# Cached-value transfers, the last cached-key scores and the last mixing product of a cross-attention stage, reordered

## The reference, cut to what matters

```python
qh = q.reshape(b, L, MEM_HEADS, MEM_HEAD_DIM)
scores = einsum('blhd,bmhd->bhlm', qh, mem_k) * MEM_HEAD_DIM ** -0.5
probs = softmax(scores, axis=-1)
o = einsum('bhlm,bmhd->blhd', probs, mem_v).reshape(b, L, MEM_DIM)
y_m = o @ w_mem_out
merged = g[:, :, 0] * y_a + g[:, :, 1] * y_b + g[:, :, 2] * y_m   # g = sigmoid of the gate projection
mix = merged @ w_o
```

## Time and profile before

| what | value |
|---|---|
| median of three runs | 1590.66 us (1589.77 to 1594.83) |
| the profiled execution, its own time | 1599.25 us |
| its span from first to last instruction | 1597.2 us |
| TensorE busy | 1478.5 us, 93% of the span |
| VectorE, ScalarE, GpSimd busy | 692.6, 455.4, 187.6 us |
| bytes moved | 368.26 MB, mean 231 GB/s |
| chain that ended last, by engine | PE 74%, DMA 17%, DVE 4%, ACT 2%, issue 2% |
| mean granted clock of TensorE | 0.969 of full speed |

### The profile page before, as it was taken

The page is one execution under the profiler, slowest core; times in us unless marked ns, Lnnn a source line. Parts: engine busy times, 40 slices in busy tenths (PEclk is TensorE's granted clock), DMA queues, the critical chain, the costliest instruction groups (busy, mean ns, idle before and its releaser), DMA issues.

```text
span 1597.2 us, 34713 instructions
## 1 busy us (share of the span) xinstructions
PE 1478.5 (93%) x14399; PEld 1190.5 (75%) x14399; DVE 692.6 (43%) x1246; ACT 455.4 (29%) x870; POOL 187.6 (12%) x360
## 2 busy tenths in 40 slices
PE   7999999999999999999999989979987887997896
PEld 7999999999988999999988769754543443443442
DVE  5766576675789472223444325564111111111114
ACT  4533545445322551223343333111100000000001
POOL 1100000000000000000000000003333233333322
PEclk9999999999999999999999989979998998999998
DMA  5232445434558332262455452966999999999994
GB/s 203 67 92 79 129 128 164 135 102 145 171 205 281 104 93 93 80 226 84 128 193 183 178 215 83 402 250 263 419 423 422 422 421 422 380 412 421 420 410 178
DMA packets 87394, 368.26 MB, mean 231 GB/s; under 512 B 14296, under 2 KB 37536, under 8 KB 72800
## 3 DMA queue, kind: packets, MB, share of 16 engines
q1 hardware_dynamic: 81120, 357.37, 59.1%
q0 software_dynamic: 6144, 8.95, 1.6%
HBM read 344.81 MB, written 29.31 MB: 234 GB/s over the span
## 4 chain that ended last, share of the span: by engine, by line
PE 74%; DMA 17%; DVE 4%; ACT 2%; issue 2%; SPq 1%; POOL 0%; POOLq 0%; DVEq 0%; ACTq 0%
PE ps L638 36%; DMA arena<-in_w 16%; PE ps L1104 8%; PE ps L782 6%; PE ps L1123 4%; PE ps L996 3%; PE ps L887 3%; PE ps L869 3%; PE ps L733 1%; PE ps L730 1%; PE ps L919 1%; PE ps L898 1%; PE ps L1088 1%; PE ps L723 1%; PE ps L1164 1%
## 5 line engine op out<-in xcount | busy, mean ns | idle before, releaser
L1104 PE MATMUL ps<-arena,xT 128*32 128x256 f32 x4096 | 254.4, 400 | 66.7 <-DMA arena<-in_w 64.7
L1104 PEld LDWEIGHTS ps<-arena,xT 128*32 128x32 f32 x4096 | 131.7, 115 | 166.3 <-issue 53.9
L1650 DVE TENSOR_TENSOR wl<-raw,wh 128x1024 fp32r<-128x1024 f32 x151 | 183.4, 1222 | 160.5 <-ACT wh L1195 160.1
L638 PE MATMUL ps<-xh,wh 128*128 128x272 f32 x1136 | 244.2, 296 | 4.6 <-DVE wl L1650 3.4
L638 PE MATMUL ps<-xh,wl 128*128 128x272 f32 x1136 | 235.5, 289 | 0.0
L638 PE MATMUL ps<-xl,wh 128*128 128x272 f32 x1136 | 235.0, 288 | 0.0
L638 PEld LDWEIGHTS ps<-xh,wh 128*128 128x128 f32 x1136 | 179.6, 189 | 15.4 <-issue 9.7
L638 PEld LDWEIGHTS ps<-xl,wh 128*128 128x128 f32 x1136 | 179.2, 189 | 0.0
L638 PEld LDWEIGHTS ps<-xh,wl 128*128 128x128 f32 x1136 | 178.1, 189 | 0.0
L1195 ACT ACTIVATE wh<-raw 128x1024 fp32r<-128x1024 f32 x151 | 158.1, 1055 | 40.4 <-PE ps L996 20.8
L2337 DVE TENSOR_TENSOR hbuf<-sg,ps 128x128 f32<-128x128 f32 x64 | 18.4, 288 | 301.0 <-ACT sg L1502 218.1
(11 more groups left out here) (428 smaller groups left out, 2352.3 us busy)
## 6 DMA issues: line engine op xcount, KB each, us to landing
arena<-in_w SPq DMA_DIRECT2D x96, 2048.0 KB
raw<-in_slabs SPq DMA_DIRECT2D x151, 512.0 KB, 4.4
bc<-acs_dram SPq DMA_DIRECT2D x16, 512.0 KB, 5.8
hs<-in_h SPq DMA_DIRECT2D x16, 512.0 KB, 5.2
out_h_sample<-hs SPq DMA_DIRECT2D x16, 512.0 KB, 4.1
kv<-in_kT SPq DMA_DIRECT2D x8, 1024.0 KB, 4.9
kv<-in_vc SPq DMA_DIRECT2D x4, 1024.0 KB, 7.8
kvx<-in_vc SPq DMA_DIRECT2D x2, 2048.0 KB, 11.9
```

The source lines that it names most:

```text
L638: r = nc.tensor.matmul(ps[:, 2 * (ub % 2) + half, 0:HT], w[:, s, col], x[:, koff + kk, half * HT:half * HT + HT], start=first and kk == 0 ...
L1104: r = nc.tensor.matmul(ps[QS * c:QS * c + QS, 2, 0:2 * FQ], xT[:, s, kk % 2, kk // 2 * QS:kk // 2 * QS + QS], arena[:, at_:at_ + 2 * FQ], ...
L1650: v.tensor_tensor(wl[:, s], raw[:, s], wh[:, s].bitcast(F32), ALU.subtract).then_inc(w_lo, 1)
```

## The change

1. Values are used in the order 0 to 7. v0 goes into slots 2 and 3 of `raw` (`v_raw`), v1 into `kv[2]`, v2 into `kv[0]`, v3 into `kv[1]`, v4 to v7 into `kvx`. The first four are issued when slab M+7 has been split (v0), after the last `scores` (v1), after `sample_scores(6)` (v2) and after `sample_scores(7)` (v3). Slabs M+10 and M+11 are loaded after `sample_values(0)`.
2. `sample_scores(7)` runs inside gate slab M+7, after its fifth block. `gather_scores(7)`, `maximum(16)` and `softmax(16)` move into the last iteration on their engines; the sample probabilities stay in `otok`.
3. The last `mix_values` writes bank 5 and doesn't wait for `low_o(6)`. `turn(16)` stands between the last two mixing products, and VectorE does `own_p(0)` and `own_p(1)` ahead of `low_o(7)`.
4. The split and remainder of slab M+10 come after the last copy of the sample rows.

```diff
-V_ORDER = (0, 1, 3, 4, 5, 6, 2, 7)
+V_ORDER = (0, 1, 2, 3, 4, 5, 6, 7)
+        v_raw = raw[:, 2:4].rearrange("p s n -> p (s n)")
...
             for k in range(KT):
+                if k < KT - 2:
+                    load(S0["M"] + RING + k)
+                    sp_.wait_ge(Z["kvb_used"], k + 1)
+                    load_kv(k + 2)
+            sp_.wait_ge(w_lo, S0["M"] + RING + KT)
+            load_v(0, v_raw, "kvb_in2")
+            sp_.wait_ge(Z["sc_mm"], MH * CHUNKS)
+            sp_.wait_ge(Z["kvb_in2"], 16)
+            load_v(1, kv[2][:], "kvb_in2")
+            sp_.wait_ge(Z["kvb_used"], NSEQ - 1)
+            load_v(2, kv[0][:], "kvb_in0")
+            sp_.wait_ge(Z["kvb_used"], NSEQ)
+            load_v(3, kv[1][:], "kvb_in1")
+            sp_.wait_ge(w_free, RING + S0["M"] + KT)
+            for half in range(2):
+                sp_.dma_start(kvx[:, 2 * half:2 * half + 2],
+                              A["vc"][4 + 2 * half:6 + 2 * half].rearrange("b p f -> p b f")).then_inc(Z["mem_vc_in" if half else "a_vc_in"], 16)
+            sp_.wait_ge(Z["kvb_used"], NSEQ + 1)
+            for k in range(KT - 2, KT):
                 load(S0["M"] + RING + k)
-                sp_.wait_ge(Z["kvb_used"], k + 1)
-                if k < NSEQ - 2:
-                    load_kv(k + 2)
-                if k == NSEQ - 2:
-                    load_kv(NSEQ + 1)
-                    sp_.wait_ge(Z["sc_mm"], MH * CHUNKS)
-                    load_kv(NSEQ)
-                    sp_.wait_ge(w_free, RING + S0["M"] + KT)
-                    for half in range(2):
-                        sp_.dma_start(kvx[:, 2 * half:2 * half + 2],
-                                      A["vc"][3 + 2 * half:5 + 2 * half].rearrange("b p f -> p b f")).then_inc(Z["mem_vc_in" if half else "a_vc_in"], 16)
-                if k == NSEQ - 1:
-                    load_kv(NSEQ + 2)
-            sp_.wait_ge(Z["kvb_used"], NSEQ + 1)
-            load_kv(NSEQ + 7)
...
+            O_BANK = (7,) * (2 * MH - 1) + (5,)
...
-                    pe.wait_ge(Z["s_own"], min(it + 1, 2 * NSEQ))
+                    pe.wait_ge(Z["s_own"], it + 1 if it < NIT - 2 else 2 * NSEQ)
+                rows_ = prob[:, it % 2] if it < NIT else otok[:]
...
-                if 2 * h + d:
-                    pe.wait_ge(Z["o_lo"], 2 * h + d)
+                if 0 < n_ < 2 * MH - 1:
+                    pe.wait_ge(Z["o_lo"], n_)
...
-                pe.wait_ge(Z["s_own"], max(b + 1, 2 * b))
+                pe.wait_ge(Z["s_own"], max(b + 1, 2 * b) if b < NSEQ - 1 else 2 * NSEQ - 1)
...
-                gate_part(k, 2, KT)
+                if k < KT - 1:
+                    gate_part(k, 2, KT)
+                else:
+                    gate_part(k, 2, 5)
+                    sample_scores(k, 2 * k)
+                    gate_part(k, 5, KT)
...
-            sample_scores(KT - 1, 2 * KT)
             mix_values(MH - 1, 0)
+            turn(NIT)
             mix_values(MH - 1, 1)
-            turn(NIT)
...
             pe.wait_ge(Z["s_own"], 3 * NSEQ + 1)
+            pe.wait_ge(Z["o_lo"], 2 * MH)
...
                 split(b + 2)
+                if k == KT - 1:
+                    softmax(NIT, otok[:])
...
             high_o(2 * MH - 2)
-            softmax(NIT, otok[:])
+            turned(NIT, PTs[:].rearrange("p m h t -> p m (h t)"))
             high_o(2 * MH - 1)
-            turned(NIT, PTs[:].rearrange("p m h t -> p m (h t)"))
...
                 low(S0["M"] + k + 2)
+                if k == KT - 1:
+                    gather_scores(k)
+                    maximum(NIT, otok[:])
...
+            normalise(NIT)
             low_o(2 * MH - 2)
-            gather_scores(NSEQ - 1)
-            maximum(NIT, otok[:])
-            normalise(NIT)
+            dve.wait_ge(Z["pt_a"], NIT + 1)
+            own_p(0)
+            own_p(1)
             low_o(2 * MH - 1)
-            dve.wait_ge(Z["pt_a"], NIT + 1)
-            for b in range(NSEQ):
+            for b in range(2, NSEQ):
                 own_p(b)
```

More of the change, by code:

```diff
@@ L513, in load_kv, with load_v @@
             def load_kv(n_):
-                slot = n_ % 2 if n_ < NSEQ else {0: 2, 1: 0, 2: 1, 7: 2}[n_ - NSEQ]
-                sp_.dma_start(kv[slot][:], A["kT" if n_ < NSEQ else "vc"][n_ % NSEQ]).then_inc(Z[f"kvb_in{slot}"], 16)
+                sp_.dma_start(kv[n_ % 2][:], A["kT"][n_]).then_inc(Z[f"kvb_in{n_ % 2}"], 16)
+            def load_v(b, dst, landed):
+                sp_.dma_start(dst, A["vc"][b]).then_inc(Z[landed], 16)
             load_kv(0)
@@ L907, in turn @@
                 if it and it % 2 == 0:
-                    pe.wait_ge(Z["s_own"], min(it + 1, 2 * NSEQ))
+                    pe.wait_ge(Z["s_own"], it + 1 if it < NIT - 2 else 2 * NSEQ)
+                rows_ = prob[:, it % 2] if it < NIT else otok[:]
                 for m in range(2):
-                    r = nc.tensor.transpose(ps[:, 6, m * P:m * P + P], prob[:, it % 2, m * P:m * P + P], ident)
+                    r = nc.tensor.transpose(ps[:, 6, m * P:m * P + P], rows_[:, m * P:m * P + P], ident)
                 r.then_inc(Z["pt_mm"], 1)
             def mix_values(h, d):
+                n_ = 2 * h + d
                 pe.wait_ge(Z["pt_a"], CHUNKS * (h + 1))
-                if 2 * h + d:
-                    pe.wait_ge(Z["o_lo"], 2 * h + d)
+                if 0 < n_ < 2 * MH - 1:
+                    pe.wait_ge(Z["o_lo"], n_)
                 for m in range(2):
-                    r = nc.tensor.matmul(ps[:, 7, :], mv[:, m, h * MHD + d * P:h * MHD + d * P + P], PT[h % 2][:, m],
+                    r = nc.tensor.matmul(ps[:, O_BANK[n_], :], mv[:, m, h * MHD + d * P:h * MHD + d * P + P], PT[h % 2][:, m],
                                          start=m == 0, stop=m == 1)
@@ L936, in sample_values @@
                 b = V_ORDER[n_]
-                if 3 <= b < 7:
-                    if b < 5:
+                if b == 0:
+                    pe.wait_ge(Z["kvb_in2"], 16)
+                    values = v_raw
+                elif b == 1:
+                    pe.wait_ge(Z["kvb_in2"], 32)
+                    values = kv[2][:]
+                elif b < 4:
+                    pe.wait_ge(Z[f"kvb_in{b - 2}"], 16 * (NSEQ // 2 + 1))
+                    values = kv[b - 2][:]
+                else:
+                    if b < 6:
                         pe.wait_ge(Z["a_vc_in"], 48)
@@ L941, in sample_values @@
                         pe.wait_ge(Z["mem_vc_in"], 32)
[L942 to L946, removed]
+                    values = kvx[:, b - 4]
                 pe.wait_ge(Z["s_own"], 2 * NSEQ + n_ + 1)
@@ L1446, in _ @@
             r.then_inc(Z["g_done"], 1)
-            split(S0["M"] + KT + 2)
             act.wait_ge(Z["pt_mm"], NIT + 2)
@@ L1450, in _ @@
                                  ps[:, 5, 0:MEM].rearrange("p (d h t) -> p d h t", d=2, h=MH), ACT.Copy).then_inc(Z["o_hi"], 1)
+            split(S0["M"] + KT + 2)
             def high_merged(k):
@@ L2032, in normalise @@
                 c_.sync()
-                v.tensor_scalar(prob[:, it % 2], prob[:, it % 2], stat[:, 3, it:it + 1], None, ALU.mult).then_inc(Z["sm_p"], 1)
+                rows_ = prob[:, it % 2] if it < NIT else otok[:]
+                v.tensor_scalar(rows_, rows_, stat[:, 3, it:it + 1], None, ALU.mult).then_inc(Z["sm_p"], 1)
             def low_o(n_):
                 dve.wait_ge(Z["o_hi"], n_ + 1)
-                v.tensor_tensor(ol[:, n_, 0:SEQ], ps[:, 7, :], oh[:, n_, 0:SEQ].bitcast(F32), ALU.subtract).then_inc(Z["o_lo"], 1)
+                v.tensor_tensor(ol[:, n_, 0:SEQ], ps[:, 7 if n_ < 2 * MH - 1 else 5, :], oh[:, n_, 0:SEQ].bitcast(F32), ALU.subtract).then_inc(Z["o_lo"], 1)
             def own(buf, src, b, used):
@@ L2096, in _ @@
             v.tensor_copy(otok[:], ps[:, 4, 0:MHD]).then_inc(Z["s_own"], 1)
-            low(S0["M"] + KT + 2)
             dve.wait_ge(Z["o_hi"], 2 * MH + 1)
@@ L2101, in _ @@
                             oh[:].rearrange("p (h d) t -> p d h t", d=2)[:, :, :, SEQ:T].bitcast(F32), ALU.subtract).then_inc(Z["o_lo"], 1)
+            low(S0["M"] + KT + 2)
             dve.sem_inc(tmp_free, KT)
```

7 lines of the change are left out of this document (4 added, 3 removed).

## The result

| | median | runs | ratio to before (95% interval) |
|---|---|---|---|
| before | 1592.97 us (1589.77 to 1599.07) | 6 | |
| after | 1585.13 us (1582.56 to 1587.21) | 6 | 0.9945 (0.9929 to 0.9960) |
| after, run again later | 1585.86 us | 6 | 0.9950 (0.9934 to 0.9965) |

The change makes the kernel 8.8 us faster by the first ratio (6.4 to 11.3) and 8.0 by the second (5.6 to 10.5). The forecast was 9.6, inside both intervals. The forecast of the level, 1581.1, is 4.0 us lower than the measured 1585.13, which lies within the whole range (1578.0 to 1586.5) but above the 1579.5 to 1583.0 that the forecast gave itself. Of the 4.0, 2.3 come from the median of before, which rose over more runs, and 1.8 from the medians, which lie 7.8 us apart and not 9.6. The spread of single executions, 4.7 us after the change and 9.3 before it, is of the size of the gain.

A forecast was written before the change was run, and what follows sets the result against it. TensorE, busy 93% of the span, was taken as the bound, with time won only in its waits and low clock. Values 6.65, transposes 0.3 and slab 2.7 sum to 9.6 us: 1590.66 to 1581.1, range 1578.0 to 1586.5.

The forecast's parts named there:

- The scores inside the slab: Gate slab M+7: 16 matmuls of `sample_scores(7)` move its end from 914.83 to about 915.93; no gain up to there.
- The second bank: Last mixing products: result 7 follows result 6 directly, from 921.7, so the values start at 923.4, 3.3 us earlier.
- Values in time: Value products: second `kvx` half lands at 929.3, values end at 931.3 instead of 937.96, 6.65 us won.
- late end: Landing of the second `kvx` half: 930.7 at the latest, which would leave 5.2 us won on the values.
- Tail and clock: Last transposes and first `w_mem_out` slab: clock holds, saving 0.3 us and 2.7 us, 3.0 in all.
- Carried to the end: After this stage: the experts' stream waits for routing, so it starts earlier by what is won, 9.6 us.
- largest term, 6.65 us: Value products: they end at 931.3 in place of 937.96.
- the late half of `kvx`: Rival: M+10 to M+13 share bandwidth, delaying the second half up to 2.4 us; only 4.0 won, 1586.7; chance 0.09.
- The slower one: Rival: late loads of M+10 and M+11 stop the slab stream, giving 1595 us or more; chance 0.04.

The follow-up runs named there:

- one bank: The changed kernel with the last mixing product back in bank 7 and the wait for `low_o(6)` restored; stage measure 33.24 us against 31.85, profiled only.
- scores behind the loop: The changed kernel with `sample_scores(7)` and its softmax moved back behind the loop; stage measure 40.07 us against 31.85, profiled only.
- transfers alone: The kernel before with only the change's value-matrix places, order and issue times, and the later split of M+10; stage measure 39.00 us against 41.56, ratio 0.9995.
- chain alone: The changed kernel with the value matrices' old places, order and issue order; stage measure 41.80 us against 41.56 before, ratio 1.0005.
- five matrices early: The changed kernel with its last iteration rearranged, part of slab M+8 multiplied early, and five value matrices issued before the gate slabs end; measure 29.34 us, ratio 0.9939.
- after again: The changed kernel, unaltered, run again beside later variants on the same chip; stage measure 33.20 us, median 1585.86 us, ratio 0.9950.
- before with filler: The kernel before with 12 extra transposes of a constant ahead of each of the last two value products; stage measure 40.14 us against 41.56, ratio 0.9967.

## Why the prediction was right

Times of after are shifted by 909.19 - 907.71 = 1.48 us onto the predicted time line.

- *The scores inside the slab.* Predicted end of the slab 915.93, measured 914.56 + 1.48 = 916.04; no wait stands ahead of them. Product 6: predicted 919.75, measured 919.86.
- *The second bank.* Product 7 predicted 921.7, measured 921.90; values predicted 923.4, measured 923.71. The start is 3.0 us earlier, where 3.3 was forecast; 1.5 of it is the bank (one bank's run), the rest the order (1.0 in the run with the scores behind the loop).
- *Values in time.* Second half predicted 929.3, measured 927.5 + 1.5 = 929.0; end of the values 929.58 + 1.48 = 931.06 against 931.3. The pace was that of the rows, 2 MB in 5.0 us. The Trainium skill (DMA: Bandwidth & Descriptors, Anatomy of one DMA, the table of fixed and variable cost) has bytes at 436 GB/s, an estimate of 4.8 us for 2 MB; here the measured 5.0 decides. The second profile, with 1.21 us of wait, has it 1.4 us later after an equal issue time, at 930.4 on the predicted time line, inside the forecast's late end of 930.7. The 929.3 was picked near the middle of 928.6 and 930.7 without a mechanism; that it falls between the two executions is partly luck.
- *Tail and clock.* Slab start predicted 933.1, measured 932.93; first slab 6.17 against 6.32. The clock stayed at 1.00 in the stage in both profiles of the changed kernel. Sum of the measure: 9.7 us in one profile, 8.4 in the other, where 9.6 was forecast.
- *Carried to the end.* The load of `x1` (`x<-in_xtok` in the profile) behind the stage is issued at 986.74, where it was at 997.95; less the shift that is 9.7 us. The timed runs confirm 8.8 (6.4 to 11.3).

What the prediction had wrong is not the sum but where it comes from. It said of the moved scores: "Up to here the change gains nothing." On TensorE that is so. But they stand behind the `kvx` transfers as the last thing that SP waits for, and without the move these leave 4 us later and 8.2 us are lost (scores behind the loop). The working had the right issue time, 916.1, and didn't say that the move is what made it possible. For the same reason its largest term, 6.65 us, can't be split into 3.3 us of chain and a rest of transfers: the transfers alone gave 2.6, the chain alone -0.2, both 9.7. And the clock's share was larger than the 3.0 named. Before, v7's product took 1.96 us instead of 1.09, which the working had booked under the values, so the low clock was 0.87 + 0.25 (transposes) + 2.56 (slab) = 3.7 us of the 9.7.

Of the rivals, the late half of `kvx` was the nearest, but not by its mechanism. In the seven profiles with the changed kernel's issue times it landed 12.3 to 13.7 us after its issue, and was late in each in which the values start as early as there or earlier: by a tenth in the first profile of the changed kernel, by 1.21 us in the second. The slower one was far off; 14 us of delay cost 0.5.

Two sums of the prediction are off without moving the forecast. The late half was priced at 2.4 us for an even split with M+10 to M+13; 2 MB beside 2 MB at the pace of the rows would be 5.0, and 2.4 is the price of 1 MB. And the lower end of the range adds up to 1590.66 - 10.2 - 2 = 1578.5, not 1578.0.

The profiled executions differ by 15.5 us of span, when the stage explains 9.7 and the time before it 1.5. Of the remaining 4.3, 3.6 lie at the very end, between the issue of the last reads of the experts' results and the first store of the output: 1584.28 - 1566.66 = 17.6 us before, 1568.82 - 1554.81 = 14.0 after. That stretch has no order by kernel, but it goes with the clock granted in it:

| profile | stretch | length us | granted clock |
|---|---|---|---|
| before | 1566.66 to 1584.28 | 17.6 | 0.81 |
| five matrices early | 1553.37 to 1571.13 | 17.8 | 0.81 |
| after again | 1555.85 to 1571.64 | 15.8 | 0.89 |
| after | 1554.81 to 1568.82 | 14.0 | 0.90 |
| one bank | 1556.45 to 1568.37 | 11.9 | 1.00 |
| before with filler | 1563.20 to 1574.97 | 11.8 | 1.00 |

All fourteen profiles fit: 11.8 to 12.0 us at 1.00 (four of them), 13.9 to 17.9 at 0.81 to 0.90 (ten). The same 16 matmuls around its start take 10.59 us before and 7.25 with one bank. So up to 6 us of a single execution's time hang on a clock fall far behind the stage, with no order by kernel, and the span of one execution can't carry a comparison of gains of this size. Which executions have the fall, and the last 0.7 us, stay open.

## What to carry to other kernels

A queue that issues its transfers from one list passes every wait on: ask of each moved piece of compute which transfers stand behind the wait that it releases, even where the move looks free on its own engine. Two changes that both end in the same join (operands ready, data landed) have no separate price; cost them together and check with each alone. When a wait near the end of a stage goes, count the low clock behind it too, here 3.7 us on top of 6.0. And when the gain is of the size of the spread between executions, compare inside the stage, on more than one profile.

## What the runs showed of the hardware

- The clock fell to 0.50 with no wait of TensorE longer than 1.40 us, after waits of 1.30 and 1.40 between short pieces. In these two stretches TensorE was busy 0.70 and 0.60 us, and the clock was 1.00 and then 0.90:

```profile
932.00:934.00 2.00, 0.70 (x16) 0.44 (x16) 0.15 (x2) 0.85 (x1) 0.00 (x0) 1.00 1.00 420
934.00:936.00 2.00, 0.60 (x16) 0.12 (x11) 0.00 (x0) 0.00 (x0) 0.00 (x0) 0.90 1.02 408
```

- With filler in those waits it fell later, within a wait of 1.03 us that followed ones of 0.59 and 0.57. In the changed kernel it held at 1.00 with waits of 0.83, 0.47, 0.56 and 0.93 us, and in the second profile with one of 1.21 more.
- A fall could be short or long: in the profile of before it lasts from 936 to beyond 944, in those of transfers only and of the filler 3 to 4 us. At the end of the kernel a fall stretched 12 us of work to up to 17.9.
- The landing of the last 2 MB varied by 1.4 us between two executions of the same kernel with the same issue times after the marker: 12.3 and 13.7 us from issue. In five other kernels with those issue times it took 12.3 to 13.0.
- A copy of 2.2 MB from memory to memory, put ahead of two loads in the queue, delayed their landing by 7 to 8.6 us; a load of 2 MB into the core lands 5.0 us behind the one before it.
